# First three cached sequences of the dilated window loaded during the mLSTM stages

## The chip, the cores and the metric

The kernel runs on one core of one Trainium2 chip. The metric is the time of one execution on the device, in microseconds; lower is better. All stages run one after the other on that core, with an all-engine barrier between them.

## The reference

One inference step of a hybrid decoder layer, for a prompt (1 x 2048 tokens) and for 8 sample sequences of 8 new tokens each, D_MODEL 1024. Each token passes a joint input projection, three mixers (mLSTM with 4 heads of 64, dilated sliding-window softmax attention with 6 heads, stick-breaking attention with 6 heads), an output projection and a squared-ReLU MLP. What matters here:

```
def mlstm_chunk(carry, xs):                 # 16 chunks of 128 prompt tokens, carried state C, n, m
    ...
    s = jnp.einsum('bhtd,bhsd->bhts', q, k) * jnp.exp(logw - m_t[..., None])
    num = w_inter[..., None] * jnp.einsum('bhed,bhtd->bhte', C, q) + jnp.einsum('bhts,bhse->bhte', s, v)
    ...
    C_new = decay[..., None, None] * C + jnp.einsum('bhs,bhse,bhsd->bhed', w_end, v, k)

def dilated_sample(q, k, v, buf_k, buf_v):  # buf_k, buf_v: 8 sequences x 2048 cached rows x 384
    k_all = jnp.concatenate([buf_k, k], axis=1)
    v_all = jnp.concatenate([buf_v, v], axis=1)
    for window, dil in ((128, 1), (512, 4), (2048, 16)):
        ...                                 # softmax over every dil-th key of the window, per branch
    return combine_branches(outs, lses), k_all[:, T:], v_all[:, T:]
```

The cached K and V of the window do not depend on anything that the kernel computes: they are inputs.

## The kernel before

`build` calls ten stages in order. Each stage is a function that opens its own SBUF and PSUM tiles and semaphores (`Mem`), writes one program per engine in a `Block`, and on leaving clears its semaphores and meets the others in an all-engine barrier (L70). Three stages matter.

**mLSTM of the prompt** (`mlstm_phase`, tiles `mq_`). After a preamble over all gates it walks 16 chunks. SP loads a chunk's keys, values and gate (`mq_X`), queries (`mq_QT`) and keys turned (`mq_KT`), three buffers deep: chunk c waits until chunk c-3 is used (L1550 to L1553). Behind the loads of chunk c SP issues `store(c-5)`, the result of an older chunk. POOL runs, for each c, `keys(c+1)`, `gate(c+1)`, `output(c)`. `output(c)` waits for DVE's `mq_HH`. ACT's `gate` is the first reader of `mq_X`. The order within each engine is written out by hand.

**mLSTM of the samples** (`mlstm_chunks(..., True)`, tiles `ms_`): one short chunk for the 64 sample tokens, some 60 us from the start of its constants to the next stage.

**Dilated attention of the samples** (`dilated_sample_phase`, tiles `sd_`). It walks the 8 sequences. Of a sequence's 2048 cached rows 1280 are loaded, in 10 tiles of 128 rows x 384: six loads of 192 KB (the far rows, 8 of every 16) and one of 768 KB (the last 512 rows), for K on SP's queue and for V on POOL's. There are three buffers of K and three of V (`NK = 3`); K of sequence b >= 3 waits for the transposes of b-3, V for `values(b-3)`. ACT's queue loads four small things first: queries, new keys, the mask (`sd_MW`) and the new values (`sd_VN`). DVE waits for all four and then scales the queries into `sd_QD`. TensorE waits for that and runs:

```
            turn(0)
            for b in range(DB):
                logits(b)
                if b + 1 < DB:
                    turn(b + 1)
                weights(b)
                if b:
                    folded(b - 1)
                values(b)
```

`turn(b)` (L2018) turns K by 30 transposes, which ACT and DVE copy out of PSUM to `sd_KT`; it waits for K's seven loads. `logits(b)` is L2028. `weights(b)` turns the weights, `values(b)` multiplies them with V.

Of the kernel before, what the change touches and what calls it, by code (L numbers as in the profile page):

```python
# [14 lines left out]
P = 128  # L15
# [4 lines left out]
NA, NB, NC = HA * HD, HB * HD, HC * HD  # L20
# [1360 lines left out]
                ins.then_inc(ok["tail"], 1)  # L1381


def mlstm_phase(nc, A, S, O):

# [6 lines left out]
    with ExitStack() as ctx:  # L1394
# [85 lines left out]
        @block.gpsimd  # L1480
        def _(pool):
            pool.memset(eps[:, :], EPS)
            pool.memset(ident[:, :], 0.0)
            pool.memset(ones[:, :], 1.0)
            pool.memset(tri[:, :], 1.0)
            pool.memset(mask[:, :], 0.0).then_inc(consts, 1)
            pool.wait_ge(consts, 1)
            pool.affine_select(out=ident[:, :], in_=ident[:, :], compare_op=ALU.not_equal, fill=1.0, base=0,
                               pattern=[[-1, P]], channel_multiplier=1)
            pool.affine_select(out=tri[:, :], in_=tri[:, :], compare_op=ALU.is_ge, fill=0.0, base=0,  # L1490
                               pattern=[[1, P]], channel_multiplier=-1)
            pool.affine_select(out=mask[:, :], in_=mask[:, :], compare_op=ALU.is_ge, fill=NEG, base=0,
                               pattern=[[1, P]], channel_multiplier=-1).then_inc(consts, 1)
            for s in range(2):
                ins = pool.memset(VX[s][:, :, :], 1.0)
            ins.then_inc(consts, 1)
            pool.wait_ge(consts, 3)
            pool.wait_ge(g_in, 16 * 4)

            def keys(c):  # L1500
                s, x = c % 2, X[c % RX]
                pool.wait_ge(x_in[c % RX], 48 * (c // RX + 1))
                if c >= 2:
                    pool.wait_ge(intra, c - 1)
                    pool.wait_ge(up_ok, c - 1)
                pool.tensor_copy(VX[s][:, :, 0:HD], x[:, 1, :, :]).then_inc(vx_ok, 1)
                if c == 0:
                    pool.wait_ge(pre_v, PRE_KS)
                pool.tensor_tensor(KW[s][:, :, :], x[:, 0, :, :], ks[:, c, :, None].broadcast_to([P, HA, HD]), ALU.mult).then_inc(kw_ok, 1)

            def gate(c):
                s = c % 2
                pool.wait_ge(og_ok, c + 1)
                if c >= 2:
                    pool.wait_ge(y2_ok, c - 1)
                pool.tensor_tensor(OM[s][:, :, :], OG[s][:, :, :], gm[:, :, :], ALU.mult).then_inc(om_ok, 1)

            def output(c):
                s = c % 2
                pool.wait_ge(om_ok, c + 1)  # L1520
                pool.wait_ge(h_ok, c + 1)
                if c >= 2:
                    pool.wait_ge(yt_ok, c - 1)
                pool.tensor_tensor(YY[s][:, :, :], HH[s][:, :, :], OM[s][:, :, :], ALU.mult).then_inc(y2_ok, 1)
                pool.wait_ge(y2_ok, c + 1)
                pool.wait_ge(rs_ok, c + 1)
                pool.tensor_tensor(YY[s][:, :, :], YY[s][:, :, :], rs[s][:, :, None].broadcast_to([P, HA, HD]), ALU.mult).then_inc(y3_ok, 1)

            keys(0)
            gate(0)  # L1530
            for c in range(NCH):
                if c + 1 < NCH:
                    keys(c + 1)
                    gate(c + 1)
                output(c)

        @block.sync
        def _(sp):
            sp.dma_start(G8[:, :, :], S["nat"][0:SEQ, GI:GI + 2 * HA].rearrange("(c p) g -> p c g", p=P)).then_inc(g_in, 16)
            sp.dma_start(bias[:, 0:HA], row_bcast(A["b_igate"], P)).then_inc(g_in, 16)  # L1540
            sp.dma_start(bias[:, HA:2 * HA], row_bcast(A["b_fgate"], P)).then_inc(g_in, 16)
            sp.dma_start(gm[:, :, :].rearrange("p h e -> p (h e)"), row_bcast(A["g_mlstm"], P)).then_inc(g_in, 16)

            def store(c):
                sp.wait_ge(yc_ok, c + 1)
                sp.dma_start(S["yT"][0:2, :, c * P:(c + 1) * P].rearrange("g p t -> p g t"), YT[c % 2][:, :, :]).then_inc(y_out[c % 2], 16)

            for c in range(NCH):
                i, cols = c % RX, slice(c * P, (c + 1) * P)
                if c >= RX:  # L1550
                    sp.wait_ge(inter, c - RX + 1)
                    sp.wait_ge(kw_ok, c - RX + 1)
                    sp.wait_ge(og_a, c - RX + 1)  # L1553
                sp.dma_start(X[i][:, :, :, :].rearrange("p a h e -> p (a h e)"), S["nat"][cols, KA:GI]).then_inc(x_in[i], 16)
                sp.dma_start(QT[i][:, :, :], S["qkT"][0:2, :, cols].rearrange("g p t -> p g t")).then_inc(x_in[i], 16)
                sp.dma_start(KT[i][:, :, :], S["qkT"][2:4, :, cols].rearrange("g p t -> p g t")).then_inc(x_in[i], 16)
                if c >= 5:
                    store(c - 5)
            for c in range(NCH - 5, NCH):
                store(c)  # L1560
            sp.wait_ge(uc_ok, 1)
            for h in range(HA):
                d0 = h % 2 * HD
                sp.dma_start(O["p_c"][h], UC[0:HD, h, d0:d0 + HD]).then_inc(o_out, 16)
                sp.dma_start(O["p_n"][h:h + 1, :], UC[HD:E1, h, d0:d0 + HD]).then_inc(o_out, 16)
            sp.dma_start(O["p_m"][0:1, :], mr[0:1, NCH, :]).then_inc(o_out, 16)
            sp.wait_ge(o_out, 16 * (2 * HA + 1))
            for s in range(2):
                sp.wait_ge(y_out[s], 16 * (NCH // 2))
# [267 lines left out]
    return ((row + row) + [rest] * (2 * DT)) * 3  # L1837


def dilated_sample_phase(nc, A, S, O):  # L1840

    PAIRS, HT_, TL, HW = 3, 2 * DT, 10, 32
    R, KEYS = PAIRS * HW, TL * P
    COLS_ = KEYS + DT
    SPANS = ((0, 4), (4, 4), (8, 2))
    NBANK = PAIRS * len(SPANS)  # L1850
    TB = ((0, 4), (4, 4), (8, 3))
    NK, FA, FV = 3, (NBANK + 1) // 2, NBANK // 2
    with ExitStack() as ctx:
        m = Mem(nc, ctx, "sd")
        K = [m.sb(f"K{i}", [P, TL, NB]) for i in range(NK)]
        V = [m.sb(f"V{i}", [P, TL, NB]) for i in range(NK)]
        KT = [m.sb(f"KT{i}", [P, PAIRS, KEYS]) for i in range(2)]
        QL = m.sb("QL", [P, PAIRS, NS])
        KN = m.sb("KN", [P, PAIRS, NS])
# [18 lines left out]
        names = ["consts", "new_in", "qd", "qdz", "kt_ps", "kt_a", "kt_v", "z", "zm", "nm", "e", "pt", "ptc_a", "ptc_v", "rd", "av", "ys", "fold", "yn", "fin", "y"]  # L1878
        ok = {x: m.sem(x + "_ok") for x in names}
        passed = m.sem("passed")  # L1880
        k_in = [m.sem(f"k_in{i}") for i in range(NK)]
        v_in = [m.sem(f"v_in{i}") for i in range(NK)]
        y_out = m.sem("y_out")
        block = ctx.enter_context(nc.Block())

        def load(eng, b, dst, src, landed):
            seq = src[b, :, :]
            far = seq[0:1536, :].rearrange("(j n r) c -> j n r c", j=6, r=16)
            for j in range(6):
                eng.dma_start(dst[b % NK][:, j, :], far[j, :, 0:8, :]).then_inc(landed[b % NK], 16)  # L1890
            eng.dma_start(dst[b % NK][:, 6:TL, :], seq[1536:WIN, :].rearrange("(j p) c -> p j c", p=P)).then_inc(landed[b % NK], 16)

        @block.gpsimd
        def _(pool):
            pool.memset(ident[:, :], 0.0)
            pool.memset(fold[:, :], 0.0).then_inc(ok["consts"], 1)
            pool.wait_ge(ok["consts"], 1)
            pool.affine_select(out=ident[:, :], in_=ident[:, :], compare_op=ALU.not_equal, fill=1.0, base=0,
                               pattern=[[-1, P]], channel_multiplier=1).then_inc(ok["consts"], 1)
            for c in range(P // HW):  # L1900
                pool.wait_ge(ok["consts"], 2 + c)
                pool.affine_select(out=fold[:, :], in_=fold[:, :], compare_op=ALU.not_equal, fill=1.0, base=-c * HW,
                                   pattern=[[-1, HW]], channel_multiplier=1).then_inc(ok["consts"], 1)
            for b in range(DB):
                if b >= NK:
                    pool.wait_ge(ok["av"], b - NK + 1)
                load(pool, b, V, A["cache_win_v"], v_in)

        @block.sync
        def _(sp):  # L1910
            for b in range(DB):
                if b >= NK:
                    sp.wait_ge(ok["kt_ps"], (b - NK + 1) * NBANK)
                load(sp, b, K, A["cache_win_k"], k_in)

        @block.scalar
        def _(act):
# [1189 lines left out]
def build(nc, A, O):  # L3107
# [11 lines left out]
    stick_prompt_phase(nc, A, S, O)  # L3119
    dilated_prompt_phase(nc, A, S, O)  # L3120
    dilated_merge_phase(nc, A, S, O)
    mlstm_phase(nc, A, S, O)
    mlstm_chunks(nc, A, S, O, True)
    dilated_sample_phase(nc, A, S, O)
    stick_sample_phase(nc, A, S, O)
    mix_out_phase(nc, A, S, O)
    mlp_phase(nc, A, S, O)
# [41 lines left out]
```

## Time and profile before

| | us |
|---|---|
| median of 3 runs | 4319.52 (4317.83 to 4326.96) |
| profiled execution, whole | 4320.33 |
| its span | 4318.9 |
| TensorE busy | 3868.3 (90%) |
| VectorE busy | 1814.8 (42%) |
| ScalarE busy | 1410.2 (33%) |
| GpSimd busy | 1010.1 (23%) |

The span is cut into 40 equal slices of 108 us in the page; a digit is the busy share in tenths. PE is TensorE's matrix multiply, PEld its weight load, DVE VectorE, ACT ScalarE, POOL GpSimd, SPq the queue of SyncE from which DMAs are issued. PEclk is the granted TensorE clock as a share of full speed. Times in the rows count from the start of the span. In a row, `[9.00 <-DMA x]` says that the engine sat idle for 9.00 us before and that the landing of x ended it. A DMA share above 1 is an artefact of overlapping packets; read it as full.

### The profile page before, as it was taken

The numbers are of one execution on the slowest core, as the hardware profiler recorded it, in microseconds if no ns is written. First come the engines' busy times: TensorE is split into PE (matmuls) and PEld (weight loads), VectorE is DVE, ScalarE is ACT, GpSimd is POOL, SyncE is SP. The second block draws the span as 40 slices with busy tenths as digits, with TensorE's granted clock in tenths as the row PEclk, the third lists the DMA queues.
The fourth block names the chain that finished last, engine by engine and source line by source line (L and its number), as shares of the span: only waits on it lengthen the run. The fifth ranks groups of instructions, "written<-read, shape, count | busy, mean of one in ns | idle before, by whom it ended". The sixth has DMA issues, their size and how long they took to land. (4 is left out here: it accounts for less than half of the span.)

```text
span 4318.9 us, 62472 instructions
## 1 busy us (share of the span) xinstructions
PE 3868.3 (90%) x22579; PEld 3248.4 (75%) x22579; DVE 1814.8 (42%) x3743; ACT 1410.2 (33%) x3007; POOL 1010.1 (23%) x1192
## 2 busy tenths in 40 slices
PE   6999998999998984383669979799999999999998
PEld 6999996343437873383446658699999999999998
DVE  2211002555555666554236654443343443433533
ACT  2311113666664452120224532223223223222222
POOL 2111002444441000131124520051150240330310
PEclk9999998999999997555779989899999999999999
DMA  4654443010002333321939955545555546546433
GB/s 167 220 179 166 163 162 118 6 35 6 8 3 86 103 118 113 95 75 43 256 125 369 362 180 173 170 129 166 181 166 177 180 141 209 160 153 216 136 117 110
DMA packets 457305, 619.63 MB, mean 143 GB/s; under 512 B 43701, under 2 KB 352566, under 8 KB 454230
## 3 DMA queue, kind: packets, MB, share of 16 engines
q1 hardware_dynamic: 415406, 481.52, 35.2%
q0 software_dynamic: 24064, 75.82, 5.0%
q10 hardware_dynamic: 17578, 58.81, 4.1%
q8 instruction: 168, 2.75, 0.3%
q14 instruction: 89, 0.73, 0.1%
HBM read 508.96 MB, written 157.20 MB: 154 GB/s over the span
## 5 line engine op out<-in xcount | busy, mean ns | idle before, releaser
L3049 PE MATMUL p_PS<-p_HI,p_WUH 128*128 128x424 f32 (+1 forms) x1280 | 457.7, 358 | 16.1 <-DVE p_WUL L2985 16.1
L3051 PE MATMUL p_PS<-p_HI,p_WUL 128*128 128x424 f32 (+1 forms) x1280 | 455.0, 355 | 0.0
L3050 PE MATMUL p_PS<-p_LO,p_WUH 128*128 128x424 f32 (+1 forms) x1280 | 453.4, 354 | 0.0
L3050 PE MATMUL p_PS<-p_UL,p_WDH 128*128 128x424 f32 (+1 forms) x1280 | 452.9, 354 | 0.0
L3049 PE MATMUL p_PS<-p_UH,p_WDH 128*128 128x424 f32 (+1 forms) x1280 | 452.7, 354 | 0.0
L3051 PE MATMUL p_PS<-p_UH,p_WDL 128*128 128x424 f32 (+1 forms) x1280 | 452.4, 353 | 0.0
L374 PE MATMUL p_PP<-p_WH,p_HH 128*128 128x384 f32 (+1 forms) x1224 | 414.1, 338 | 27.3 <-DVE p_WL L305 27.3
L2995 DVE TENSOR_TENSOR p_WDL<-p_WD,p_WDH 128x512 fp32r<-128x512 f32 x320 | 221.2, 694 | 455.0 <-ACT p_WDH L2928 455.0
L375 PE MATMUL p_PP<-p_WL,p_HH 128*128 128x384 f32 (+1 forms) x1224 | 406.8, 332 | 0.0
L376 PE MATMUL p_PP<-p_WH,p_HL 128*128 128x384 f32 (+1 forms) x1224 | 406.5, 332 | 0.0
L2873 POOL CAST p_WUH<-p_WU 128x1024 fp32r<-128x1024 f32 x160 | 168.7, 1054 | 931.6 <-PE p_PS L3051 535.4
L2928 ACT ACTIVATE p_WDH<-p_WD 128x512 fp32r<-128x512 f32 x320 | 201.1, 631 | 488.2 <-PE p_PS L3051 480.4
L2985 DVE TENSOR_TENSOR p_WUL<-p_WU,p_WUH 128x1024 fp32r<-128x1024 f32 x160 | 211.4, 1323 | 325.9 <-POOL p_WUH L2873 325.9
L464 POOL TENSOR_TENSOR pc_SL<-pc_SL,pc_L 128x512 f32<-128x512 f32 (+3 forms) x216 | 232.1, 1090 | 200.8 <-DVE pc_L L548 200.8
L295 ACT ACTIVATE p_PT<-p_PP,p_rs 128x384 f32<-128x384 f32 (+1 forms) x153 | 87.2, 570 | 549.6 <-PE p_PP L376 549.6
L2919 ACT ACTIVATE p_R<-p_PS 128x424 f32<-128x424 f32 (+1 forms) x160 | 83.8, 524 | 547.3 <-PE p_PS L3051 547.3
L3049 PEld LDWEIGHTS p_PS<-p_HI,p_WUH 128*128 128x128 f32 x1280 | 241.2, 188 | 21.5 <-issue 16.5
L374 PEld LDWEIGHTS p_PP<-p_WH,p_HH 128*128 128x128 f32 x1224 | 231.5, 189 | 30.7 <-DVE p_WL L305 23.7
L3051 PEld LDWEIGHTS p_PS<-p_HI,p_WUL 128*128 128x128 f32 x1280 | 241.2, 188 | 7.5
L3050 PEld LDWEIGHTS p_PS<-p_LO,p_WUH 128*128 128x128 f32 x1280 | 241.4, 189 | 6.0
L3049 PEld LDWEIGHTS p_PS<-p_UH,p_WDH 128*128 128x128 f32 x1280 | 240.6, 188 | 5.2
L3051 PEld LDWEIGHTS p_PS<-p_UH,p_WDL 128*128 128x128 f32 x1280 | 240.5, 188 | 5.2
(427 smaller groups left out, 7223.6 us busy)
## 6 DMA issues: line engine op xcount, KB each, us to landing
p_WU<-in_w_up SPq DMA_DIRECT2D x160, 512.0 KB, 4.1
p_WD<-in_w_down SPq DMA_DIRECT2D x320, 256.0 KB, 2.7
sc_KP<-in_cache_sb_k SPq DMA_DIRECT2D x256, 192.0 KB, 5.3
sc_VP<-in_cache_sb_v POOLq DMA_DIRECT2D x256, 192.0 KB, 5.7
pb_X<-scratch_nat SPq DMA_DIRECT2D x48, 576.0 KB, 3.6
out_s_wk<-in_cache_win_k ACTq DMA_DIRECT2D x64, 382.5 KB
out_s_wv<-in_cache_win_v ACTq DMA_DIRECT2D x64, 382.5 KB
p_HH<-scratch_xh SPq DMA_DIRECT2D x34, 512.0 KB, 4.5
```

Source lines behind the costliest of these rows:

```text
L295: act.activation(PT[v % 2][:, a - o:e - o], PP[(3 * v + b) % 4][:, 0:e - a], ACT.Copy, scale=rs[:, t:t + 1]).then_inc(blk_ok, 1)
L374: pe.matmul(out, HH[s][:, k, :], wh, start=(k == 0), stop=False)
L375: pe.matmul(out, HH[s][:, k, :], wl, start=False, stop=False)
L376: ins = pe.matmul(out, HL[s][:, k, :], wh, start=False, stop=(k == KD - 1))
L464: ins = pool.tensor_tensor(new[:, a:CH], old[:, a:CH], L[u % 4][:, a:CH], ALU.add)
L2873: pool.tensor_copy(WUH[u % RU][:, :, :], WU[u % RU][:, :, :]).then_inc(wh_ok, 1)
L2928: act.activation(WDH[g % RS][:, :], WD[:, g % RD, :], ACT.Copy).then_inc(dh_ok, 1)
L2985: dve.tensor_tensor(WUL[u % RU][:, :, :], WU[u % RU][:, :, :], WUH[u % RU][:, :, :].bitcast(F32), ALU.subtract).then_inc(wl_ok, 1)
L2995: dve.tensor_tensor(WDL[g % RS][:, :], WD[:, g % RD, :], WDH[g % RS][:, :].bitcast(F32), ALU.subtract).then_inc(dl_ok, 1)
L3049: pe.matmul(out, hi, rhi, start=first, stop=False)
L3050: pe.matmul(out, hi, rlo, start=False, stop=False)
L3051: return pe.matmul(out, lo, rhi, start=False, stop=last)
```

## The change

The three K and three V buffers move out of the dilated stage's `Mem` into a `CachedWindow`, opened before the prompt's mLSTM stage and closed behind the dilated stage, with the six semaphores of their loads. The loads of sequences 0 to 2 are issued in the prompt's mLSTM stage: V of sequence c by POOL between `gate(c+1)` and `output(c)` for c = 0, 1, 2; K of sequences 0, 1, 2 by SP at the end of its turns c = 6, 9, 12, behind `store(c-5)`. The dilated stage issues only sequences 3 to 7, behind the same waits as before. Each load is the same seven DMAs.

```diff
+class CachedWindow:
+    NK, TL = 3, 10
+
+    def __init__(self, nc, ctx):
+        m = Mem(nc, ctx, "cw")
+        self.K = [m.sb(f"K{i}", [P, self.TL, NB]) for i in range(self.NK)]
+        self.V = [m.sb(f"V{i}", [P, self.TL, NB]) for i in range(self.NK)]
+        self.k_in = [m.sem(f"k_in{i}") for i in range(self.NK)]
+        self.v_in = [m.sem(f"v_in{i}") for i in range(self.NK)]
+
+    def load(self, eng, b, dst, src, landed):
+        i, seq = b % self.NK, src[b, :, :]
+        far = seq[0:1536, :].rearrange("(j n r) c -> j n r c", j=6, r=16)
+        for j in range(6):
+            eng.dma_start(dst[i][:, j, :], far[j, :, 0:8, :]).then_inc(landed[i], 16)
+        eng.dma_start(dst[i][:, 6:self.TL, :], seq[1536:WIN, :].rearrange("(j p) c -> p j c", p=P)).then_inc(landed[i], 16)
...
@@ mlstm_phase, GpSimd
                 if c + 1 < NCH:
                     keys(c + 1)
                     gate(c + 1)
+                if c < W.NK:
+                    W.load(pool, c, W.V, A["cache_win_v"], W.v_in)
                 output(c)
@@ mlstm_phase, SyncE
                 if c >= 5:
                     store(c - 5)
+                if c in (6, 9, 12):
+                    W.load(sp, c // 3 - 2, W.K, A["cache_win_k"], W.k_in)
@@ dilated_sample_phase
-        K = [m.sb(f"K{i}", [P, TL, NB]) for i in range(NK)]
-        V = [m.sb(f"V{i}", [P, TL, NB]) for i in range(NK)]
+        K, V, k_in, v_in = W.K, W.V, W.k_in, W.v_in
...
-            for b in range(DB):
-                if b >= NK:
-                    pool.wait_ge(ok["av"], b - NK + 1)
-                load(pool, b, V, A["cache_win_v"], v_in)
+            for b in range(NK, DB):
+                pool.wait_ge(ok["av"], b - NK + 1)
+                W.load(pool, b, V, A["cache_win_v"], v_in)
...
-            for b in range(DB):
-                if b >= NK:
-                    sp.wait_ge(ok["kt_ps"], (b - NK + 1) * NBANK)
-                load(sp, b, K, A["cache_win_k"], k_in)
+            for b in range(NK, DB):
+                sp.wait_ge(ok["kt_ps"], (b - NK + 1) * NBANK)
+                W.load(sp, b, K, A["cache_win_k"], k_in)
@@ build
-    mlstm_phase(nc, A, S, O)
-    mlstm_chunks(nc, A, S, O, True)
-    dilated_sample_phase(nc, A, S, O)
+    with ExitStack() as ctx:
+        W = CachedWindow(nc, ctx)
+        mlstm_phase(nc, A, S, O, W)
+        mlstm_chunks(nc, A, S, O, True)
+        dilated_sample_phase(nc, A, S, O, W)
```

## Rows read from the trace of the kernel before

**Rows 1.** The page, 40 slices: TensorE's busy tenths.

```profile
PE   6999998999998984383669979799999999999998
```

**Rows 2.** Busy time by stretch, columns as in the first line.

```profile
core 0: us, PE busy (x) PEld busy (x) DVE busy (x) ACT busy (x) POOL busy (x), PEclk, DMA share, GB/s
1810.00:1970.00 160.00, 139.67 (x654) 128.85 (x653) 85.12 (x255) 44.94 (x140) 47.34 (x75) 0.50 0.23 66
2041.30:2064.40 23.10, 0.00 (x0) 0.00 (x0) 1.39 (x3) 1.28 (x1) 13.23 (x28) 0.50 0.99 260
...
2071.70:2100.80 29.10, 17.26 (x137) 11.91 (x137) 5.30 (x11) 4.39 (x8) 0.00 (x0) 0.65 1.08 277
2100.80:2118.20 17.40, 14.17 (x141) 8.56 (x139) 6.22 (x13) 4.39 (x8) 3.92 (x7) 0.90 0.83 240
2187.20:2204.30 17.10, 13.91 (x140) 8.32 (x139) 6.22 (x13) 4.39 (x8) 0.00 (x0) 0.90 0.00 1
```

**Rows 3.** Waits from 2041 to 2101: total us, times, longest.

```profile
PE sd_KTP L2018 <- DMA sd_K<-in_cache_win_k: 42.6, 2, 33.6
```

**Rows 4.** Timeline: start us, us, engine line operation, out<-in, count, idle before.

```profile
2050.35 0.71 DVE L1951 TENSOR_SCALAR sd_QD<-sd_QL 64x192 f32<-64x192 f32 x2 [8.14 <-DMA sd_VN<-scratch_nat]
...
2064.46 2.46 PE L2018 MATMUL sd_KTP<-sd_ident,sd_K 128*128 128x128 f32 x10 [33.63 <-DMA sd_K<-in_cache_win_k]
...
2071.74 2.35 PE L2028 MATMUL sd_ZP<-sd_KT,sd_QD 128*32 128x512 f32 x18 [0.47 <-ACT sd_KT L1928]
...
2083.13 2.49 PE L2018 MATMUL sd_KTP<-sd_ident,sd_K 128*128 128x128 f32 x10 [9.00 <-DMA sd_K<-in_cache_win_k]
...
2100.84 2.35 PE L2028 MATMUL sd_ZP<-sd_KT,sd_QD 128*32 128x512 f32 x18
...
2118.26 2.35 PE L2028 MATMUL sd_ZP<-sd_KT,sd_QD 128*32 128x512 f32 x18
```

**Rows 5.** Timeline: the mask and VN; landings of like loads elsewhere.

```profile
2042.28 0.50 ACTq L1920 DMA_DIRECT2D sd_MW<-in_window_mask  x1
2042.81 0.35 ACTq L1921 DMA_DIRECT2D sd_VN<-scratch_nat  x1
...
DMA to landing us min/median/max: 2.4/2.4/2.4
...
p_WU<-in_w_up SPq DMA_DIRECT2D x160, 512.0 KB, 4.1
```

**Rows 6.** All loads of sd_K: from issue to landing.

```profile
DMA to landing us min/median/max: 2.8/7.5/28.5
```

**Rows 7.** Issues of V0 and V3 on POOL, of K0 and K2 on SP.

```profile
2041.28 3.82 SPq L1890 DMA_DIRECT2D sd_K<-in_cache_win_k  x6
...
2043.75 3.20 POOL L1890 DMA_DIRECT2D sd_V<-in_cache_win_v  x6 [0.34 <-issue]
...
2056.94 18.66 SPq L1890 DMA_DIRECT2D sd_K<-in_cache_win_k  x6
...
2101.21 3.15 POOL L1890 DMA_DIRECT2D sd_V<-in_cache_win_v  x6 [45.62 <-PE sd_YP L2066]
```

**Rows 8.** Timeline of POOL: output(0) and output(1) with the idle before.

```profile
1819.40 0.90 POOL L1524 TENSOR_TENSOR mq_YY<-mq_HH,mq_OM 128x256 f32<-128x256 f32 x1 [6.76 <-DVE mq_HH L1712]
...
1828.45 0.90 POOL L1524 TENSOR_TENSOR mq_YY<-mq_HH,mq_OM 128x256 f32<-128x256 f32 x1 [5.37 <-DVE mq_HH L1712]
```

**Rows 9.** Chunk 7's load and its first reader; landings of mq_X.

```profile
1849.14 0.35 SPq L1554 DMA_DIRECT2D mq_X<-scratch_nat  x1
...
1868.13 0.40 ACT L1580 ACTIVATE mq_OG<-mq_X 128x256 f32<-128x256 f32 x1
...
DMA to landing us min/median/max: 3.0/3.1/5.1
```

**Rows 10.** Last output, its landing, and the next stage's first instruction.

```profile
2228.48 0.95 ACTq L1941 DMA_DIRECT2D scratch_yT<-sd_YA  x2
...
scratch_yT<-sd_YA ACTq DMA_DIRECT2D x2, 96.0 KB, 1.9
...
2231.89 0.26 SPq L2230 DMA_DIRECT2D sc_table<-in_page_table  x1
```

More of the change, by code:

```diff
@@ L1381, in _, with mlstm_phase @@
                 ins.then_inc(ok["tail"], 1)
-def mlstm_phase(nc, A, S, O):
+class CachedWindow:
[12 more added lines that the diff above has]
+        eng.dma_start(dst[i][:, 6:self.TL, :], seq[1536:WIN, :].rearrange("(j p) c -> p j c", p=P)).then_inc(landed[i], 16)
+def mlstm_phase(nc, A, S, O, W):
     E1, NCH, RX = HD + 1, NT, 3
@@ L1837, in window_masks, with dilated_sample_phase @@
     return ((row + row) + [rest] * (2 * DT)) * 3
-def dilated_sample_phase(nc, A, S, O):
-    PAIRS, HT_, TL, HW = 3, 2 * DT, 10, 32
+def dilated_sample_phase(nc, A, S, O, W):
+    PAIRS, HT_, TL, HW = 3, 2 * DT, W.TL, 32
     R, KEYS = PAIRS * HW, TL * P
@@ L1851, in dilated_sample_phase @@
     TB = ((0, 4), (4, 4), (8, 3))
-    NK, FA, FV = 3, (NBANK + 1) // 2, NBANK // 2
+    NK, FA, FV = W.NK, (NBANK + 1) // 2, NBANK // 2
     with ExitStack() as ctx:
         m = Mem(nc, ctx, "sd")
-        K = [m.sb(f"K{i}", [P, TL, NB]) for i in range(NK)]
-        V = [m.sb(f"V{i}", [P, TL, NB]) for i in range(NK)]
+        K, V, k_in, v_in = W.K, W.V, W.k_in, W.v_in
         KT = [m.sb(f"KT{i}", [P, PAIRS, KEYS]) for i in range(2)]
@@ L1880, in dilated_sample_phase @@
         passed = m.sem("passed")
-        k_in = [m.sem(f"k_in{i}") for i in range(NK)]
-        v_in = [m.sem(f"v_in{i}") for i in range(NK)]
         y_out = m.sem("y_out")
         block = ctx.enter_context(nc.Block())
[L1886 to L1891, printed above, removed]
         @block.gpsimd
```

## The prediction

> **What bounds the kernel now.** I read the page first: over the span TensorE is the busy engine, but its busy share by slices falls to 3, 6 and 6 tenths in the three slices from 1943 to 2267 [rows 1], and an average says nothing of a stretch like that. So I took the stretches one by one [rows 2]. In the mLSTM stage (1810 to 1970) the DMA engines are 23% busy. In the sample tokens' dilated stage the picture turns over: for 23.1 us TensorE does nothing at all while the DMA engines are 0.99 busy, and the first sequence's iteration (29.1 us) holds 17.26 us of TensorE work with the DMA engines full. Behind it stand six iterations of 17.1 to 17.4 us; the first has a DMA share of 0.83, the last of 0.00: their length does not follow the transfers.
>
> The waits name the cause [rows 3]: TensorE's transposes of K waited 42.6 us, in two waits, for `sd_K<-in_cache_win_k`. The timeline has the dates [rows 4]: turn(0) starts at 2064.46, logits(0) at 2071.74, turn(1) at 2083.13 after 9.00 us of idling, logits(1) at 2100.84, logits(2) at 2118.26; QD was scaled at 2050.35, after 8.14 us of waiting for the last of four small loads.
>
> **The first wait.** With K0 to K2 and V0 to V2 in SBUF before the stage, turn(0) waits only for POOL's constants, a few us, and for QD, which needs those four loads on ACT's queue. The last, VN, is issued at 2042.81; a load of its size with no bulk load ahead landed in 2.4 us: 2045.2. The mask (483 KB) is issued at 2042.28, and loads of 512 KB landed in a median of 4.1 us: 2046.4 [rows 5]. Then 0.71 us of scaling and some 0.1 us of handover: turn(0) at 2047.2 instead of 2064.46, a gain of 17.3 us. Bounds: QD as late as before (2050.35 + 0.81 = 2051.2) leaves 13.3 us; a mask that lands no later than VN (2046.0) gives 18.5 us.
>
> **The second wait.** logits(0) to logits(1) took 29.10 us; the same code from logits(1) to logits(2) took 17.42 us with K and V at hand [rows 4]. So 11.7 us are to be had at the clock of the later iterations (0.90). The clock was not there at once: iteration 0 had 0.65 [rows 2]. Were it again as slow as after its 9 us pause (2100.84 − 2083.13 = 17.71, plus 2.3 of logits), it would take 20.0 us, and 9.1 us remain. Now turn(0), logits(0) and turn(1) follow each other without that pause, so I stay near the fast end and take 10.7 us.
>
> What is late next? Sequences 3 to 7 still load inside the stage. K3 goes out when turn(0) ends, about 2054.5, and is wanted by turn(3), behind logits(2), about 2091: 36 us. V3 goes out after values(0), about 2072.5, and is wanted by values(3), about 2120: 47 us. The longest landing of a K load was 28.5 us, with three sequences of K and V in the queues at once [rows 6]. A sequence's K and V are 3.93 MB, at 260 to 277 GB/s 14.2 to 15.1 us against an iteration of 17.3 us. The six later iterations keep their length: nothing there.
>
> **What the loads cost in the mLSTM stage.** V: POOL spends 3.20 us on six issues and some 4.1 us on a sequence's seven [rows 7]. They stand between gate(c+1) and output(c) of c = 0, 1, 2, where POOL idled 6.76 and 5.37 us for DVE (the third gap lies between) [rows 8]: covered, with 1.3 us to spare in the tightest. K: SP spends 3.82 us on six issues, some 4.5 us on the seven [rows 7], behind store(1), store(4) and store(7); what stands behind them in SP's queue are the three loads of chunk 7 (10, 13). Those went out at 1849.14, landed 3.1 us later, and ACT's gate read them first, at 1868.13 [rows 9]. Even if issue and drain of K0 (1.97 MB, 7.6 us at 260 GB/s) began only at 1849.14, chunk 7 would be in by 1864.3: 3.8 us left. I take 0, with 3 us as the upper end (one load of each kind a little late). Below nothing: no instruction of that stage goes away, so a gain has no source.
>
> **The exit.** One more clear of semaphores with an all-engine barrier follows the stage. From the landing of the last output (issued by 2228.9, 1.9 us) to the next stage's first instruction 1.1 us passed [rows 10], for the block's end, a clear and a barrier; I take 0.5, bounds 0 and 1.0.
>
> Sum: −17.3 − 10.7 + 0 + 0.5 = −27.5 us. On the profiled execution's 4320.33 us (span 4318.9 and 1.4 outside it) this gives 4292.8; that execution lies 0.8 above the median of the runs shown, so the median comes to **4292.0 us**. With all bounds together the gain is 18.4 to 30.2 us: 4301 to 4289.
>
> **Rivals.** A: each of POOL's seven issues waits for a DVE instruction. DVE is busy 85.12 of 160 us there, over 255 instructions of 0.33 us on average [rows 2]; with two of them per issue a load takes 4.1 + 4.7 = 8.8 us, which overruns the three gaps by 2.0, 3.4 and some 2.5 us: 8 us if nothing behind absorbs it, 4300. Against it: six of POOL's later issues, beside a DVE that was 36% busy, took 3.15 us, as much as the first six [rows 2, 7]. 5%. The Trainium skill, SBUF — State Buffer (§ SBUF: two separate sides), states such a rule: POOL writes a DMA's descriptors through a port that certain vector instructions lock for their whole length, so the transfer stalls behind them. By that rule the time would go towards 4300, by the rows it stays at 4292.
>
> B: the loads of sequences 3 to 7 become the wait, since computing starts earlier than they do. If five of them come 2 to 4 us late, 10 to 20 us are lost: 4302 to 4312. For it: the DMA engines were full until 2100. Against it: 36 and 47 us of lead against 28.5 at most. 6%, half of it too large to leave a gain.
>
> C, slower than before: chunk inputs are held behind the cache loads in SP's queue. The slack from issue to reader is 19.0 − 3.1 = 15.9 us. It starts to cost when a K load holds the queue longer than that, the gain is gone at 15.9 + 27.5/3 = 25.1 us, and at 30 us 3 × 14.1 = 42 us are lost: 4334. For it: the landing of 28.5 us and SP's six issues that took 18.66 us [rows 6, 7]. Against it: both fell into the pile-up of three K and three V loads; here each K load is alone and the next is 30 us away. 3%.
>
> The forecast has 86%. Faster and slower count from 0.2% (8.6 us), about what a measurement of this kernel tells from no change: faster 0.94, within 0.03, slower 0.03. The range 4288 to 4301 holds the forecast with nearly all of its bounds, and rival A.
>
> **What would show it.** Right: `sd_KTP` waits for `sd_K` in neither place; turn(0) is released by QD about 6 us into the stage; logits(0) to logits(1) 17.4 to 18.5 us; six periods of 17.1 to 17.5; mLSTM chunks as far apart as before; the stage some 28 us shorter than 190.6. Wrong: POOL's output(c) of chunks 0 to 2 late, a wait of ACT or TensorE for `mq_X` or `mq_KT` at chunks 7, 10 or 13, or a wait for cache loads at sequence 3 or 4. Later iterations that shift by more than 2 us in all would be an effect of the clock that the sum does not hold.

## The result

The changed kernel took **4301.1 us** (median of 5 runs, 4297.93 to 4303.01); the kernel before, run beside it, 4325.12 (5 runs, 4317.83 to 4326.96). The ratio is 0.9945, with a 95% interval of 0.9934 to 0.9956: a gain of 23.8 us, between 19.0 and 28.5. A second set of the same two kernels gave 0.9952 (0.9938 to 0.9965), a gain of 20.8 us. The forecast was 4292.0 us, with a range that ended at 4301, and a gain of 27.5 us. The kernel is faster, but the time lies just above the range.

The waits of 2044 to 2078 in the profiled execution after (engine, operation, releaser: total us, times, longest). The two waits for K [rows 3] are gone. One wait is left at `sd_KTP`, and QD ends it:

```profile
PE sd_KTP L2030 <- DVE sd_QD L1963: 17.4, 1, 17.4
```

Its timeline (start us, us, engine, line, operation; in brackets the idle time before and its releaser), first the mLSTM stage with the loads that moved into it, then the dilated stage, which begins at 2044.5:

```profile
1816.16 3.19 POOL L1400 DMA_DIRECT2D cw_V<-in_cache_win_v  x6
...
1823.00 0.89 POOL L1544 TENSOR_TENSOR mq_YY<-mq_HH,mq_OM 128x256 f32<-128x256 f32 x1 [2.85 <-DVE mq_HH L1736]
...
1832.04 0.89 POOL L1544 TENSOR_TENSOR mq_YY<-mq_HH,mq_OM 128x256 f32<-128x256 f32 x1 [1.45 <-DVE mq_HH L1736]
...
1849.99 3.85 SPq L1400 DMA_DIRECT2D cw_K<-in_cache_win_k  x6
...
1854.59 0.43 SPq L1576 DMA_DIRECT2D mq_X<-scratch_nat  x1
...
1871.71 0.40 ACT L1604 ACTIVATE mq_OG<-mq_X 128x256 f32<-128x256 f32 x1
...
2046.03 0.35 ACTq L1933 DMA_DIRECT2D sd_VN<-scratch_nat  x1
...
2051.06 0.71 DVE L1963 TENSOR_SCALAR sd_QD<-sd_QL 64x192 f32<-64x192 f32 x2 [5.61 <-DMA sd_VN<-scratch_nat]
...
2051.87 2.46 PE L2030 MATMUL sd_KTP<-sd_ident,cw_K 128*128 128x128 f32 x10 [17.37 <-DVE sd_QD L1963]
...
2059.89 2.35 PE L2040 MATMUL sd_ZP<-sd_KT,sd_QD 128*32 128x512 f32 x18 [0.47 <-ACT sd_KT L1940]
...
2077.04 2.35 PE L2040 MATMUL sd_ZP<-sd_KT,sd_QD 128*32 128x512 f32 x18
...
2182.06 2.35 PE L2040 MATMUL sd_ZP<-sd_KT,sd_QD 128*32 128x512 f32 x18
...
2198.56 10.41 PE L2104 MATMUL sd_PTP<-sd_ident,sd_YN 16*128 16x16 f32 x48 [0.64 <-DVE sd_YN L1982]
...
2209.77 0.95 ACTq L1953 DMA_DIRECT2D scratch_yT<-sd_YA  x2
...
2213.55 0.25 SPq L2242 DMA_DIRECT2D sc_table<-in_page_table  x1
```

The stretches of [rows 2] in the kernel after (from:to, length, busy us with counts of PE, PEld, DVE, ACT, POOL; granted clock, DMA share, GB/s): the mLSTM stage, one of the middle iterations, the last iteration, and the closing stretch:

```profile
1813.50:1973.50 160.00, 139.73 (x654) 128.92 (x654) 85.02 (x255) 45.04 (x140) 59.15 (x96) 0.50 0.46 140
...
2077.00:2094.40 17.40, 14.18 (x141) 8.54 (x139) 6.22 (x13) 4.40 (x8) 4.00 (x7) 0.90 0.77 230
...
2163.30:2182.00 18.70, 15.52 (x141) 9.13 (x139) 6.22 (x13) 4.39 (x8) 0.00 (x0) 0.82 0.00 1
2182.00:2213.50 31.50, 22.38 (x161) 16.82 (x159) 5.65 (x13) 1.95 (x3) 0.00 (x0) 0.65 0.03 7
```

What the reader is to see: the DMA engines' share in the mLSTM stage doubled, 0.23 to 0.46, and TensorE's busy time there is the same 139.7 us. In the dilated stage the gain came at the front, and something was given back at the back.

Worked out from such timelines, one profiled execution for each kernel (us; "mLSTM stage" is both mLSTM stages together, prompt and samples; turn(0) and L0, the start of logits(0), are counted from the dilated stage's first instruction; L0-L1 is the first iteration, "six" the six iterations from logits(1) to logits(7), "closing" the time from logits(7) to the next stage):

```
kernel   span    mLSTM  turn(0)  L0      L0-L1  six     closing  dilated
                 stage  at       at                              stage
before   4318.9  258.0  +23.18   +30.46  29.10  103.50  27.55    190.61
after    4301.5  257.7   +7.35   +15.37  17.15  105.02  31.49    169.03
```

The span is 17.4 us shorter: the dilated stage gave 21.6 and the mLSTM stages 0.3, while the stages ahead of both took 3.5 us more (they end at 1786.8 against 1783.3) and those behind 0.9 more. No instruction ahead of the mLSTM stage was changed, and other executions of the kernel before reached that point at 1788.2 and 1782.5, so the 3.5 us are a difference between executions; what causes it I did not settle.

### The profile page after: what moved, and what is told of

Read it like the earlier page. It is cut to its first block and busy times, and to the rows that moved or that the text cites. A ratio compares the mean times of both kernels' runs of the same rounds, so it can differ in the third digit from the quotient of the medians.

```text
span 4301.5 us, 62485 instructions
## 1 busy us (share of the span) xinstructions
PE 3871.5 (90%) x22579; PEld 3250.4 (76%) x22579; DVE 1815.2 (42%) x3743; ACT 1411.1 (33%) x3007; POOL 1011.5 (24%) x1192
## 5 line engine op out<-in xcount | busy, mean ns | idle before, releaser
L374 PE MATMUL p_PP<-p_WH,p_HH 128*128 128x384 f32 (+1 forms) x1224 | 414.1, 338 | 27.5 <-DVE p_WL L305 27.5
```

The source lines that it names most:

```text
L374: pe.matmul(out, HH[s][:, k, :], wh, start=(k == 0), stop=False)
```

## The experiments

Three sets of runs, each beside runs of the kernel before, whose medians were 4323.07 (9 runs), 4321.36 (9) and 4323.69 (19). The forecast stood on the 4319.52 of three runs. A "low spell" below is a stretch in which TensorE's granted clock is at the lower of its two levels, 0.50.

**The same kernel again, and one half of the change at a time.** First the kernel after, unchanged; then V's loads alone in the mLSTM stage; then K's alone:

```diff
 V early alone, in SP's mLSTM loop:
-                if c in (6, 9, 12):
-                    W.load(sp, c // 3 - 2, W.K, A["cache_win_k"], W.k_in)
 and in its dilated stage:
-            for b in range(NK, DB):
-                sp.wait_ge(ok["kt_ps"], (b - NK + 1) * NBANK)
+            for b in range(DB):
+                if b >= NK:
+                    sp.wait_ge(ok["kt_ps"], (b - NK + 1) * NBANK)
 K early alone, in POOL's mLSTM loop (and the dilated one alike):
-                if c < W.NK:
-                    W.load(pool, c, W.V, A["cache_win_v"], W.v_in)
```

> The changed kernel as it is, a second time. In its first profile the dilated stage of the samples took 169.0 us from its first instruction to the next stage's, 6 us more than the 163.1 forecast, and 5.5 us of that arose behind logits(1): the clock was at its low level for 6 to 7 us at a time in the last two iterations and in the closing matmuls, where it had been low for 3 to 4 us at a time before. Theory P (where the clock's low spells fall is a matter of how the stage happens to lie, and varies from execution to execution): the stretch from logits(7) to the next stage comes out between 27.5 and 31.5 us, and need not be 31.5 again. Theory S (the loss belongs to the change, since the loads end earlier): 31.5 us again, stage 169. Ratio to before 0.9935 to 0.9956 by both.

> Only V of sequences 0 to 2 is loaded in the mLSTM stage; K0 to K2 are loaded at the dilated stage's start as before, now without V beside them. Theory Q (the waits came from three K and three V loads sharing the engines): K0, 1.97 MB at about 260 GB/s, is in by 9 to 11 us into the stage against 23.2 before and 7.4 with both early; K1 by 18 and K2 by 26 us, both ahead of their transposes (about 20 and 37 us), so the stage is 2 to 4 us longer than with both early and some 18 to 20 us shorter than before; ratio about 0.9955. Theory K (K must be early, a K load takes its time alone too): turn(0) starts 18 us or more into the stage and less than half of the gain is left, ratio 0.998 or more.

> Only K of sequences 0 to 2 is loaded in the mLSTM stage; V0 to V2 are loaded at the dilated stage's start by GpSimd. V0 is wanted 27 us into the stage and 1.97 MB take about 10 us, so no wait for V. The four small loads share the engines with V: QD between 6.5 us (as with both early) and 9.1 us (as before) into the stage. Theory Q: stage 0 to 2.5 us longer than with both early, ratio 0.9945 to 0.9952. Rival: V early is what frees the start (the small loads), then QD at 9 us or later and the stage over 3 us longer, ratio 0.9955 or more.

Measured: 4303.14 for the same kernel, ratio 0.9952; V early alone 4305.23, 0.9959 (0.9945 to 0.9972); K early alone 4302.45, 0.9952 (0.9938 to 0.9965). Their profiled dilated stages: 170.3, 175.7 and 167.1 us; the last is 2.0 us shorter than the kernel after's, where 0 to 2.5 longer was expected, and the repeat shows below that executions differ by as much. K early alone brings the whole gain; V early on top of it adds nothing that can be measured. But V early alone has most of it as well: turn(0) began at +13.94, later than my +9 to 11, and its stage was 6.6 us longer than with both early where I had expected 2 to 4; it is still 9 us before the +23.18 of the kernel before, from which it differs by the three V loads that no longer shared the queues. Its second wait for K was gone too (L0-L1 17.17). What cost 42.6 us in [rows 3] was six loads at once, and taking away either three does most of the work.

The repeat shows something else. Same code, other places: its L0-L1 took 19.39 instead of 17.15, its next iteration 20.94 instead of 17.40, its last iteration 17.15 instead of 18.72, its closing stretch 27.86 instead of 31.49. Windows of its first two iterations:

```profile
2059.20:2078.60 19.40, 15.50 (x137) 9.29 (x137) 5.21 (x11) 4.39 (x8) 0.00 (x0) 0.76 0.65 205
2078.60:2099.50 20.90, 18.20 (x140) 10.45 (x139) 6.22 (x13) 4.39 (x8) 3.99 (x7) 0.70 0.61 189
```

As many instructions as elsewhere, the same DVE, ACT and POOL time; TensorE takes longer for the same count, and the granted clock is 0.70 where a 17.40 us iteration has 0.90. No wait for a load stands in them.

**The clock as its own cause.** Theory: each iteration has a place where TensorE pauses, behind it the granted clock falls to its lower level (0.50, that is 1.2 GHz) for a while, and how long differs from execution to execution. In 2 us windows of the iteration of the kernel after that starts at 2077:

```profile
2086.00:2088.00 2.00, 0.78 (x8) 0.70 (x8) 0.28 (x2) 1.17 (x2) 0.00 (x0) 1.00 0.60 164
2088.00:2090.00 2.00, 1.96 (x19) 0.91 (x18) 0.87 (x3) 0.49 (x1) 0.00 (x0) 0.70 1.01 300
2090.00:2092.00 2.00, 2.00 (x40) 1.69 (x39) 0.63 (x2) 0.00 (x0) 0.00 (x0) 0.50 1.01 267
2092.00:2094.00 2.00, 2.00 (x30) 1.06 (x19) 0.00 (x0) 0.00 (x0) 0.00 (x0) 0.95 0.81 288
```

TensorE waits, 1.82 us for ScalarE's exponential, and soon after it the clock is granted at 0.50 (1.2 GHz) for some 3 us though TensorE is then busy throughout. If that holds, moving the stage in time should move or remove spells, and filling the pause should remove them all. The rival: the longer iterations come from the loads. The shift puts a memset between the small loads and QD:

```diff
             dve.wait_ge(ok["new_in"], 64)
+            dve.memset(PAD[:, :], 0.0)
```

> The changed kernel with one idle memset of 128x2048 on VectorE between the landing of the small loads and the scaling of the queries: turn(0) and all behind it start about 1.8 us later, nothing else differs. Theory P (the place of the clock's low spells depends on how the stage lies in time): the stretch behind logits(1), 136.5 us in the changed kernel and 131.1 before, moves by more than 1.5 us either way and the stage is not simply 1.8 us longer (anywhere from 3 us shorter to 4 us longer). Theory S (the loss belongs to the earlier loads): 136.5 us again, stage 170.8 us, time 1.8 us more than the changed kernel's.

It took 4300.98 us, ratio 0.9949 (0.9936 to 0.9963). turn(0) began 2.0 us later than in the kernel after, at +9.40, and the stage was 1.9 us shorter, 167.1. Its second and third iterations:

```profile
2080.50:2096.30 15.80, 12.57 (x140) 7.53 (x139) 6.22 (x13) 4.39 (x8) 3.99 (x7) 1.00 0.74 228
2096.30:2115.10 18.80, 15.61 (x143) 9.43 (x143) 6.22 (x13) 4.39 (x8) 3.92 (x7) 0.82 0.76 229
```

15.80 us with no low spell, then 18.80 with a long one, at the same DMA share: not the loads. One execution cannot show that the memset did this, only that such lengths occur.

The kernel before was asked the same. Two more profiles of it:

> The kernel before, a second profile. The forecast stood on one profiled execution of it, 4320.33 us; its dilated stage took 190.6 us with one low spell of 3 to 4 us of the clock in each iteration. Theory P (the clock's low spells differ from execution to execution, and that first profile was a good draw): the stage comes out between 188 and 196 us and the stages ahead of the mLSTM between 1780 and 1790 us. Theory S (the kernel before is steady, only the changed one loses to the clock): stage 190.6 within 0.5 us and logits(7) to the next stage 27.6 us.

> The kernel before, a third profile, for the same question: theory P, a stage that differs from the other two profiles' by 1 us or more, with the difference in the iterations' lengths (15.8, 17.1 to 17.4, 18.7 or 20.9 us, as seen so far) and in the closing 48 matmuls; theory S, 190.6 us again.

Their dilated stages took 190.33 and 193.91 us (4326.01 and 4322.72 in all). In the first, the six iterations and the closing stretch repeated those of the forecast's profile to 0.02 us each, as S said; in the second they did not, as P said. The second had L0-L1 26.92 and then an iteration of 20.92; in that one the same 18 logits matmuls that take 2.35 us elsewhere took nearly twice that:

```profile
2072.59 2.35 PE L2028 MATMUL sd_ZP<-sd_KT,sd_QD 128*32 128x512 f32 x18 [0.47 <-ACT sd_KT L1928]
...
2099.51 4.49 PE L2028 MATMUL sd_ZP<-sd_KT,sd_QD 128*32 128x512 f32 x18
```

The lengths are not scattered, though. In all ten profiles without filler, of either kernel and its variants, most of the seven iterations form one run that shrinks in the same order from 17.4 to 17.1 us (17.42, 17.37, 17.25, 17.17, 17.14, 17.15 in the forecast's profile), and only one to three iterations before or behind that run have another length. What differs between executions is where the run begins.

**Filling the pause.** Twelve transposes of the identity into a PSUM tile that is free by then, before the wait for the exponential (24 in the last iteration, whose pause is 3.30 us), and QD's wait moved behind turn(0) in a kernel of its own:

```diff
 fill:
+                if b:
+                    pe.wait_ge(ok["ptc_v"], 2 * b)
+                for _ in range(12 if b + 1 < DB else 24):
+                    pe.transpose(PTP[0][:, 0:P], ident[:, :], ident[:, :])
                 pe.wait_ge(ok["e"], b + 1)
 ... (the wait for ptc_v inside the loop behind it goes)
 QD later:
-            pe.wait_ge(ok["qd"], 1)
             turn(0)
+            pe.wait_ge(ok["qd"], 1)
```

> The changed kernel with TensorE's wait for ScalarE's exponential filled: ahead of each weights(b) 12 transposes of the identity (24 in the last sequence, where the wait is 3.3 us instead of 1.8) into the PSUM tile that weights(b) overwrites next. Nothing reads them. Theory P (each iteration pays for a low spell that begins behind that idle stretch): the spells go, the iterations take 15.8 to 16.1 us (the one iteration without a spell in the shifted kernel took 15.82), the stage 8 to 14 us less than 169 to 171, time 4289 to 4294, ratio about 0.9925. Rival F (the clock falls for another reason, the filler only adds work): iterations stay at 17.1 us or get longer, time 4301 or more.

> The changed kernel with TensorE's wait for the scaled queries moved from before turn(0) to behind it: turn(0) needs only K and the identity. turn(0) then starts about 2.3 us into the stage (the constants) instead of 7.4, is done at about 10.3, and logits(0) starts there instead of at 15.4 to 15.7, since the queries are ready at 7.3: 5 us less, stage 164 to 166, time about 4297, ratio 0.9935. Rival: the gain is lost again to where the clock's low spells fall, time 4300 or more.

The filler gave 4287.98 us, ratio 0.9921 (0.9907 to 0.9934), although it adds work. It gave more than I had expected (a stage 8 to 14 us shorter, 4289 to 4294 us): all seven iterations took 15.82 or 15.83 us, the six 94.95 (105.02 after), the stage 152.2 (169.0). One iteration, and the filler with the pause that it leaves, to be set beside the windows above:

```profile
2072.80:2088.60 15.80, 13.88 (x153) 8.82 (x152) 6.22 (x13) 4.40 (x8) 3.99 (x7) 1.00 0.81 251
```

```profile
2080.97 1.47 PE L2050 MATMUL sd_PTP<-sd_ident 128*128 128x128 f32 x12
2082.95 0.88 PE L2061 MATMUL sd_PTP<-sd_ident,sd_Z 96*128 96x96 f32 x8 [0.51 <-ACT sd_Z L1948]
...
2085.27 1.72 PE L2080 MATMUL sd_YP<-cw_V,sd_PT 128*32 128x128 f32 x52
```

The same stretch in the kernel after; the 52 matmuls of values(b) need 3.29 us there and 1.72 with the filler:

```profile
2087.22 0.88 PE L2059 MATMUL sd_PTP<-sd_ident,sd_Z 96*128 96x96 f32 x8 [1.82 <-ACT sd_Z L1948]
...
2089.54 3.29 PE L2078 MATMUL sd_YP<-cw_V,sd_PT 128*32 128x128 f32 x52
```

So 1.6 us of an iteration of 17.4 was the clock's. The loads keep up at this pace as well: no wait for them appears.

QD later gave 4297.91, ratio 0.9945 (0.9931 to 0.9958), a stage of 163.4, both near what was expected; but not by the step expected. turn(0) began at +2.19 and then stood waiting for DVE, whose first copy of K was queued behind QD's scaling:

```profile
2047.41 2.49 PE L2030 MATMUL sd_KTP<-sd_ident,cw_K 128*128 128x128 f32 x10 [12.21 <-POOL sd_fold L1916]
...
2051.74 0.71 DVE L1963 TENSOR_SCALAR sd_QD<-sd_QL 64x192 f32<-64x192 f32 x2 [5.60 <-DMA sd_VN<-scratch_nat]
...
2053.23 5.15 PE L2030 MATMUL sd_KTP<-sd_ident,cw_K 128*128 128x128 f32 x20 [3.33 <-DVE sd_KT L1971]
```

logits(0) came at +13.68, 1.7 us earlier than in the kernel after; most of the rest of its shorter stage is a closing stretch of 27.88 instead of 31.49.

**The early loads with the clock out of the way, the moved code without them, and the best version.** The filler once more on the kernel after; the same filler on the kernel before; the changed kernel with its buffers where they are and all its loads inside the dilated stage; and the filler, QD later, and on DVE the scaling behind the first copies:

```diff
 best, DVE's queue (besides the two edits above):
-            dve.wait_ge(ok["qdz"], 1)
-            dve.wait_ge(ok["new_in"], 64)
-            ... (the scaling of QD)
             keys(0)
+            dve.wait_ge(ok["qdz"], 1)
+            dve.wait_ge(ok["new_in"], 64)
+            ... (the scaling of QD)
 moved only, in the mLSTM loops of POOL and SP:
-                if c < W.NK:
-                    W.load(pool, c, W.V, A["cache_win_v"], W.v_in)
-                if c in (6, 9, 12):
-                    W.load(sp, c // 3 - 2, W.K, A["cache_win_k"], W.k_in)
 ... (in the dilated stage both loops run over all b again, as above)
```

> The filled kernel again, beside the one with the earlier turn(0) and the kernel before with the filler. Theory P: iterations 15.82 us and the stage 152.2 us within 1 us again, since with no low spell in the iterations nothing is left in the stage that varies; time 4284 to 4290. Rival: the stage varies by 2 us or more, as that of the changed kernel did.

> The kernel before (loads of sequences 0 to 2 at the stage's start) with the same filler. Theory P: its six later iterations, 103.5 to 107.3 us in three profiles, take 6 x 15.82 = 94.9 us, the closing stretch 27 us, the first two waits stay, and the stage takes 181 to 184 us against 190.4 to 193.9. The early loads are then worth 29 to 32 us between the two filled kernels (152.2 us), against the 20 to 25 us between the unfilled ones, and near the forecast's 27.5. Rival (the shorter iterations run into the loads, 3.93 MB in 15.8 us being 249 GB/s): waits for K or V at sequences 3 to 5, iterations of 16.5 us or more, stage 186 or more.

> The buffers live from the mLSTM stage on as in the changed kernel, but all loads are issued in the dilated stage as before. It prices the exit alone: one more clear and barrier, 0.4 us (from the last output's issue to the next stage 2.83 us against 2.46). Stage between 190.4 and 195, as the three profiles of before, ratio 0.999 to 1.001. Rival (tiles that live over three stages cost by themselves, or the gain is from their place in SBUF and not from the early loads): ratio beyond 1.002 or below 0.998.

> The filled kernel, with turn(0) ahead of the queries on TensorE, and on VectorE the copies of turn(0) ahead of the scaling of the queries (in the kernel that moved TensorE's wait alone, turn(0) stalled 3.33 us on VectorE's first copy, which stood behind the scaling). turn(0) starts 2.2 us into the stage and takes 8.0 us at the low clock, logits(0) starts at about 10.8 instead of 14.45, iterations 15.82 us, stage about 148.5 against 152.2, time 3.7 us below the filled kernel's. Rival: the small loads or the scaling become the last to arrive, logits(0) at 12 us or later and under 2.5 us gained.

```
kernel             median us  ratio to before (95%)    turn(0)  L0      L0-L1  six     closing  dilated
after + filler     4284.15    0.9909 (0.9893, 0.9924)   +7.49   +15.55  15.83   94.93  28.33    154.6
before + filler    4310.57    0.9973 (0.9963, 0.9983)  +23.69   +31.64  26.88   94.95  25.71    179.2
moved only         4324.54    1.0004 (0.9995, 1.0013)  +24.74   +32.38  26.20  103.76  27.84    190.2
best               4279.43    0.9899 (0.9884, 0.9914)   +2.19   +10.04  15.83   94.95  26.71    147.5
```

Moving the code and the buffers does nothing that can be measured: the effect is in the loads' dates. The two filler rows are the comparison that the forecast described, with the six iterations equal on both sides: logits(1) comes at 58.52 without early loads and at 30.31 or 31.38 with them, 27.1 to 28.2 us sooner (forecast 17.3 + 10.7 = 28.0); the closing stretch gives 1.3 to 2.6 back; the stages differ by 24.5 to 27.0 and the medians by 26.4. With the first filled kernel's 4287.98, from another set of runs, the medians differ by only 22.6, no more than without filler; so that the early loads are worth more with filler rests on the profiled stages and on one set of medians. My expectations for them were too narrow: the two executions with the same filler differ by 2.4 us (I had said within 1; the rival had 2 or more), all of it ahead of logits(0) and in the closing stretch, and the kernel before with it had a stage of 179.2, where 181 to 184 was expected. Its iterations ran at full clock with the queues full, and waited for the cache loads only in the two places of [rows 3], once more 42.4 us in all:

```profile
2099.20:2115.00 15.80, 13.89 (x152) 8.85 (x151) 6.22 (x13) 4.39 (x8) 3.93 (x7) 1.00 1.02 260
```

The best version, 4.7 us below the filled kernel where 3.7 was expected, takes 44 us off the kernel before, against some 21 to 24 of the change as it was. DVE's first copy no longer waits behind QD, and QD arrives just behind the copies:

```profile
2046.81 2.49 PE L2030 MATMUL sd_KTP<-sd_ident,cw_K 128*128 128x128 f32 x10 [12.19 <-POOL sd_fold L1916]
...
2053.90 0.70 DVE L1983 TENSOR_SCALAR sd_QD<-sd_QL 64x192 f32<-64x192 f32 x2
2054.66 2.35 PE L2040 MATMUL sd_ZP<-sd_KT,sd_QD 128*32 128x512 f32 x18 [0.71 <-DVE sd_QD L1983]
```

## Why the prediction was off, step by step

**The first wait: mechanism right, 1.5 us too much.** turn(0) was released by QD, at +7.35 instead of +5.9; the gain was 15.8 us (23.18 − 7.35), inside the bounds of 13.3 to 18.5. DVE went on 5.0 us after VN's issue (2046.03 to 2051.06); I had put the last landing 3.6 us behind that issue. The records of the DMA packets on ACT's queue in this execution tell the two loads apart by size: the mask's 96 packets (5152 bytes each) ran from 2046.63 to 2049.11 and VN's 64 (1536 bytes each) from 2048.07 to 2049.67, so VN was the later. VN did not have the 2.4 us of [rows 5], as its packets stood behind the mask's, and the last update of the loads' semaphore came at 2050.96, 1.3 us after the last packet. With K early, QD was scaled at +6.5 to +7.2 in every execution except those of the two kernels that delay it; with K loading inside the stage, at +9.1 to +9.4.

**The second wait: mechanism right, its size in part luck.** logits(0) to logits(1) took 17.15 us, so 12.0 were gained where 10.7 was forecast and 11.7 was the bound; in the repeat it was 19.39, a gain of 9.7. The allowance for the clock was of the right size, but both sides vary more than it held: without the wait and without filler five more executions had 19.39, 19.20, 18.43, 18.26 and (V early alone) 17.17, and the kernel before had 29.10, 28.85 and 26.92, of which the forecast knew the longest. turn(0) to logits(0) took 8.02 instead of 7.28, at the low clock. Together this brought 27.0 us in the profiled execution (59.56 to 32.52 at logits(1)), 1.0 short of the 28.0; in the repeat logits(1) came 2.5 us later, at 35.06.

**The step that failed: "The six later iterations keep their length: nothing there."** Nothing waits in them, as argued, but they took 1.5 us more in the profiled execution, 3.8 more in the repeat, and the closing stretch, of which the forecast said nothing and which it so took as unchanged, 3.9 more (31.49 against 27.55), of which the exit is 0.4. That stretch's 48 small matmuls took 10.41 us; in the profile of before they took

```profile
2219.46 8.23 PE L2092 MATMUL sd_PTP<-sd_ident,sd_YN 16*128 16x16 f32 x48 [0.64 <-DVE sd_YN L1970]
```

and the granted clock was 0.65 against 0.76. These 5.5 us (1.52 and 3.94) are what the stage gave less than its front: 21.6 us against 27.0. Against the 163.1 us that the sum gives for the stage, the 5.9 too many are 1.5 for QD, 0.7 up to logits(0), −1.2 in the first iteration, 1.5 in the six and 3.4 in the closing stretch beyond the exit's forecast 0.5. In the repeat, 7.2 us too many, the largest term was the six iterations, 3.8. The forecast took the 17.1 to 17.5 us of [rows 2] for the length of an iteration. It is 15.82 plus what low spells of no fixed length add: iterations of the same code came as 15.82, 17.1 to 17.4, 18.7 and 20.9. The text named an effect of the clock on later iterations as a thing outside its sum; it belonged in the range, with some 3 to 6 us. Whether the early loads themselves bring the longer spells, or these executions only drew them, is not shown: the kernel before had such an iteration in one profile of three.

**The baseline.** 4319.52 was the median of three runs; the later medians of the same kernel lie at 4321.4 to 4325.1. A gain of 27.5 us from 4323.7, the median of 19, would have been 4296.2. So of the 9 us between 4292.0 and 4301.1 about 4 are the reference and about 5 are gain not had (4 to 7 by the two ratios). In the profiled executions the 10.2 us too many (4303.01 against 4292.8) are 5.9 in the dilated stage, 3.5 ahead of the mLSTM stage, 0.9 behind, 0.1 outside the span, less 0.3.

**The loads in the mLSTM stage: nothing, as forecast.** V's seven issues took 3.19 + 0.85 us on POOL, output(0) still waited 2.85 us for DVE after them, output(1), the tightest, 1.45 where 1.3 was forecast, and the two mLSTM stages together took 257.3 to 258.4 us in all fourteen profiled executions, early loads or none. K0's seven issues held chunk 7's load back until 1854.59; its first reader ran at 1871.71, 17.1 us later, so rival C's slack shrank by 1.9 us of 19.0 and no more. Landings of `cw_K` in the kernel after took 6.1 us at most (28.5 for `sd_K` in [rows 6]).

**The exit** took 2.83 us from the end of the last output's issue to the next stage's first instruction, 2.46 before [rows 10]: +0.4 for a forecast of 0.5. The moved code, which has the same exit, came to 1.0004.

**Rivals.** A did not happen: six issues took 3.19 us, 3.20 in [rows 7]. But its condition was hardly put to the test in the mLSTM stage. DVE is busy there for 85 of 160 us, and the issues fell where it mostly waits itself, 2.61 busy us of the 11.94 that the three sequences' issues took:

```profile
1816.16:1820.16 4.00, 4.00 (x22) 3.67 (x21) 0.79 (x3) 0.00 (x0) 3.99 (x8) 0.50 0.86 248
1826.62:1830.59 3.97, 3.97 (x23) 3.75 (x23) 1.22 (x3) 0.53 (x2) 3.97 (x8) 0.50 0.87 245
1835.66:1839.63 3.97, 3.97 (x23) 3.75 (x24) 0.60 (x2) 0.00 (x0) 3.97 (x8) 0.50 0.86 265
```

That was luck, not foresight: the price of A was worked out from DVE's average. Beside a DVE that was busy for 1.81 of 3.93 us, in the dilated stage from 2094.81, six issues took 3.16 us. The Trainium skill, SBUF — State Buffer (§ SBUF: two separate sides), says that POOL cannot write a DMA's descriptors while certain vector instructions hold the port that the two share; the 3.19 and 3.16 us show none of it for the few vector instructions that ran beside them, and no run here shows what a denser DVE would do. V's loads of 192 KB landed in the mLSTM stage in 3.9 us in the median and K's, from SP, in 3.2; no run says why. B is refuted by the kernels with the filler: iterations 1.6 us shorter and still no wait for a load of sequences 3 to 7. Its 4302 to 4312 was nearly the measured time for a wrong reason, which the traces tell apart. C did not happen.

Open: what makes a low spell some 3 us long in most iterations and some 7 in others, why the closing stretch takes 25.7 us in one execution and 31.5 in another, and where the 3 to 5 us between executions ahead of the mLSTM stage come from.

## What to carry to other kernels

Where a stage opens with its queues full and its main engine idle, try to start loads in an earlier stage with spare queues. Here either half of them was worth most of the gain, and it cost nothing measurable, since each issue fell into idle time or slack of the issuing engine. Before an iteration's length is taken as a constant, split it by the granted clock in short windows: here a pause of 2 us was paid for twice, once as idle time and once at the lower clock behind it, and a dozen dummy transposes took the second part away. A forecast of 0.6% needs a baseline of more than three runs, and in a queue that runs in order a wait moved away on one engine must be moved on the engines that feed it too.

## What was not expected of the hardware

A pause of TensorE of 1.82 us, in iterations of 17.4 us with 14.18 busy, was followed in nearly every iteration by 3 us or more at the granted clock of 0.50 (one iteration with the same pause had none); 1.47 us of filler that left 0.51 us of pause kept it at 1.00, and the stage fell from 169 to 152 and 155 us. In the mLSTM stage the clock stayed at 0.50 although TensorE was busy for 139.7 of 160 us. The loads kept up with the faster consumer: 260 GB/s at a share of 1.02 in a 15.8 us iteration, with no wait for a load after the first two.
